# HGRN stage: the projection between the level products in whole chunks at every second place

## What is computed

```
z = RMSNorm_pre(x) @ w_in                      # one projection, 13312 columns
f = lb + (1 - lb) * sigmoid(bf);  k = 1 - f    # per head: bf, bq, bi, bg are 128 columns each of z
S_t = diag(f_t) S_{t-1} + k_t (x) i_t
o_t = S_t^T q_t
y_b = RMSNorm_head(o) * silu(bg)
```

## Time and profile before

| | |
|---|---|
| median of three runs | 1952.8 us |
| profiled execution, whole time | 1953.2 us |
| its span on the core | 1951.4 us |
| TensorE (PE) matmul busy | 1892.8 us, 97% of the span |
| VectorE (DVE) busy | 726.9 us, 37% |
| GpSimd (POOL) busy | 477.7 us, 24% |
| ScalarE (ACT) busy | 354.8 us, 18% |
| TensorE clock granted, mean | 0.989 |

### The profile page before, as it was taken

The page is one execution under the profiler, slowest core; times in us unless marked ns, Lnnn a source line. Parts: engine busy times, 40 slices in busy tenths (PEclk is TensorE's granted clock), DMA queues, the critical chain, the costliest instruction groups (busy, mean ns, idle before and its releaser), DMA issues. The chain is left out here.

```text
span 1951.4 us, 34705 instructions
## 1 busy us (share of the span) xinstructions
PE 1892.8 (97%) x13648; PEld 1827.3 (94%) x13648; DVE 726.9 (37%) x1247; ACT 354.8 (18%) x855; POOL 477.7 (24%) x276
## 2 busy tenths in 40 slices
PE   7999999999999999999999999998999999999796
PEld 6999999999999999999999999998999999999795
DVE  6223123213223325755675665466000412221423
ACT  5121221122022111011011111112111211111221
POOL 2221222221222122222122221232333333332220
PEclk9999999999999999999999999999999999999898
DMA  5424315223333321112122112134322322223512
GB/s 155 118 67 97 100 50 119 84 67 71 104 89 63 92 75 46 54 56 60 39 67 67 34 54 67 35 123 142 99 66 66 104 90 74 75 73 117 181 33 91
DMA packets 245775, 159.18 MB, mean 82 GB/s; under 512 B 35133, under 2 KB 232125, under 8 KB 245692
## 3 DMA queue, kind: packets, MB, share of 16 engines
q1 hardware_dynamic: 207820, 124.16, 22.4%
q10 hardware_dynamic: 37872, 33.79, 5.3%
HBM read 123.48 MB, written 34.44 MB: 81 GB/s over the span
## 5 line engine op out<-in xcount | busy, mean ns | idle before, releaser
L232 PE MATMUL psum<-x_hi,w_hi 128*128 128x384 f32 (+1 forms) x2688 | 886.6, 335 | 20.7 <-DVE x_lo L2126 10.6
L232 PE MATMUL psum<-x_lo,w_hi 128*128 128x384 f32 (+1 forms) x2688 | 868.0, 327 | 0.0
L232 PEld LDWEIGHTS psum<-x_hi,w_hi 128*128 128x128 f32 x2688 | 507.2, 189 | 38.3 <-issue 22.6
L232 PEld LDWEIGHTS psum<-x_lo,w_hi 128*128 128x128 f32 x2688 | 507.9, 189 | 0.0
L232 PE MATMUL psum<-x_hi,w_lo 128*128 128x384 f32 (+1 forms) x2688 | 498.0, 326 | 0.0
L206 POOL CAST w_hi<-w_raw 128x1024 fp32r<-128x1024 f32 (+1 forms) x136 | 145.2, 1068 | 1420.3 <-PE psum L232 1089.2
L232 PEld LDWEIGHTS psum<-x_hi,w_lo 128*128 128x128 f32 x2688 | 451.4, 188 | 0.0
L208 POOL TENSOR_TENSOR w_lo<-w_raw,w_hi 128x1024 fp32r<-128x1024 f32 (+1 forms) x136 | 332.3, 2443 | 10.9
L1569 ACT ACTIVATE a_feature<-psum 128x384 f32<-128x384 f32 (+1 forms) x100 | 45.2, 452 | 355.1 <-PE psum L232 355.1
L1681 DVE TENSOR_TENSOR a_prob<-psum,band 128x128 f32<-128x128 f32 (+1 forms) x64 | 21.5, 378 | 205.2 <-PE psum L1375 203.9
L246 ACT ACTIVATE c_ext<-psum 128x384 f32<-128x384 f32 (+1 forms) x96 | 45.1, 473 | 243.7 <-PE psum L232 234.7
(11 more groups left out here) (226 smaller groups left out, 1792.6 us busy)
## 6 DMA issues: line engine op xcount, KB each, us to landing
w_raw<-in_w_in SPq DMA_DIRECT2D x104, 512.0 KB, 3.9
s_cached<-in_cache_kv_w SPq DMA_DIRECT2D x128, 64.0 KB, 2.6
s_cached<-in_cache_kv_w SPq DMA_DIRECT2D x64, 128.0 KB, 2.4
merged_rows<-c_ext ACTq DMA_DIRECT2D x15, 544.0 KB, 3.0
a_feature<-group_weights SPq DMA_DIRECT2D x12, 512.0 KB, 5.9
spare<-branch_outputs SPq DMA_DIRECT2D x10, 544.0 KB, 6.3
branch_outputs<-b_gate ACTq DMA_DIRECT2D x8, 544.0 KB, 3.1
c_ext<-merged_rows SPq DMA_DIRECT2D x8, 544.0 KB, 3.7
```

Of the source, the lines that this page charges most:

```text
L232: mm = pe.matmul(psum[:, c, 0:n], w[:, s, k, :], x[:, k, t0:t0 + n], start=step is first, stop=step is last)
```

## The change

Only the numbers of halves between the steps of a head change. `counts` is (before, levels, own, out, turn, after).

```diff
                         with pe.Fori(0, BH - 1) as i:
-                            head(i, (1, (1, 1, 1, 1, 2, 1, 1, 1), 2, 4, 5, 3))
-                        head(BH - 1, (1, (1, 1, 1, 1, 2, 1, 1, 1), 3, 5, 6, 0))
+                            head(i, (2, (0, 2, 0, 2, 2, 0, 2, 0), 2, 4, 6, 2))
+                        head(BH - 1, (2, (0, 2, 0, 2, 2, 0, 2, 0), 4, 4, 6, 0))
```

## The result

The changed kernel takes 2019.55 us (median of four runs, 2018.34 to 2024.42), the kernel before 1952.93 us. The forecast was 2006 us with a range of 1996 to 2019. The direction was right. The size was short by 13.5 us of 66.6, and the time lies just above the range. The profiled execution took 2018.34 us, with a span of 2016.5 us.

A forecast was written before the change was run, and what follows sets the result against it. TensorE's in-order list was taken to bound the HGRN stage. Per head 7.17 + 0.35 - 0.70 - 0.19 = 6.63 us, 53 us over eight heads, added to 1953.2 us: forecast 2006 us, range 1996 to 2019.

The forecast's parts named there:

- What bounds the kernel: HGRN stage: TensorE busy 68.91 of 69 us per head, so no slack in which a new stall could vanish.
- Part 1, the four waits: Behind levels 0, 2, 5 and 7 TensorE waits for VectorE's updates: 1.65, 2.06, 1.74, 1.72 us, together 7.17 us per head.
- Part 2, the saved change-overs: Whole-chunk places: four fewer projection visits save 0.70 us per head; the 0.19 us wait ahead of level 6 also disappears.
- Part 3, GpSimd: Levels 4 to 5: GpSimd's subtraction delays update(4), a stall of 0.35 us per head, between 0 and 0.77.
- the first rival, the clock: TensorE's clock falls at the new waits, one fall per head at 1.5 us, 12 us, giving 2018 us; chance 14%.
- The range: Whole time: 1996 us for stalls mis-sized by a fifth, up to 2019 us for one clock fall per head.

The follow-up runs named there:

- levels 0 and 1 alone: Kernel before with nothing behind level 0 and two halves behind level 1, all other places unchanged: 1968.48 us, ratio 1.0084.
- the waits gone: Changed kernel with level products and transposes of k reading constant tiles, so they wait for no update (right data left out): 1944.8 us, ratio 0.9969.
- the kernel with the bare pair 5 and 6: Kernel before with nothing behind level 5 and two halves behind level 6, all other places unchanged: 1984.66 us, ratio 1.0169.
- the kernel with less filler: Changed kernel with three filler matmuls, about 0.6 us, in each of the four bare places: 2009.76 us, ratio 1.0294 to the kernel before.

## Why the prediction was wrong

**What bounds the kernel: right.** TensorE's list had no slack. The length of a head followed the waits and change-overs (levels 0 and 1 alone: 1.38 us more expected, 1.38 found).

**Part 1, the four waits: right.** Timeline of TensorE in the head with full clock, to lay beside the earlier trace rows:

```profile
875.07 1.26 PE L887 MATMUL psum<-b_q_new,b_k_decayed 128*64 128x64 f32 x34
877.88 1.23 PE L887 MATMUL psum<-b_q_decayed,b_k_decayed 128*64 128x32 f32 x34 [1.56 <-DVE b_q_decayed L1040]
883.41 1.24 PE L887 MATMUL psum<-b_q_decayed,b_k_decayed 128*64 128x32 f32 x34
886.62 1.23 PE L887 MATMUL psum<-b_q_decayed,b_k_decayed 128*64 128x32 f32 x34 [1.97 <-DVE b_k_decayed L1053]
891.49 1.12 PE L887 MATMUL psum<-b_q_decayed,b_k_decayed 128*64 128x32 f32 x32
896.93 1.13 PE L887 MATMUL psum<-b_q_decayed,b_k_decayed 128*64 128x32 f32 x32
899.72 1.12 PE L887 MATMUL psum<-b_q_decayed,b_k_decayed 128*64 128x32 f32 x32 [1.66 <-DVE b_k_decayed L1053]
905.16 1.15 PE L882 MATMUL psum<-b_q_decayed,b_k_decayed 128*64 128x64 f32 x16
907.94 1.20 PE L896 MATMUL psum<-ident,b_k_decayed 128*128 128x128 f32 x9 [1.63 <-DVE b_k_decayed L1053]
```

| from start to start | forecast | measured |
|---|---|---|
| level 0 to 1 | 2.84 | 2.81 |
| level 2 to 3 | 3.23 | 3.21 |
| level 5 to 6 | 2.79 | 2.79 |
| level 7 to k | 2.80 | 2.78 |

The idle times in brackets are about 0.08 us shorter than the forecast stalls, since they count from the recorded end of a product and the forecast from 0.07 us before it.

**Part 2, the saved change-overs: right.** In the changed kernel the four distances hold 7.10 us of stall (11.59 less the products' own 4.49), and a head with full clock is 6.19 us longer, so 0.91 us were saved, against 0.70 + 0.19 forecast. With the waits gone the order alone gives 0.55 us per head, or 0.83 without the new wait of `own_states`, against 0.70.

**Part 3, GpSimd: the meeting came, the 0.35 us did not.** Level 4 to 5 took 896.93 - 891.49 = 5.44 us, not 5.8. Timelines of VectorE and of GpSimd, the same head:

```profile
892.66 0.62 DVE L1049 TENSOR_TENSOR b_block_decay<-b_block_decay 128x64 f32<-128x64 f32 x1 [0.36 <-PE psum L887]
893.20 0.68 DVE L1051 TENSOR_TENSOR b_q_decayed<-b_q_decayed,b_block_decay 128x512 f32<-128x512 f32 x1
893.80 2.89 DVE L1053 TENSOR_TENSOR b_k_decayed<-b_k_decayed,b_block_decay 128x512 f32<-128x512 f32 x1
```
```profile
893.28 2.86 POOL L208 TENSOR_TENSOR w_lo<-w_raw,w_hi 128x1024 fp32r<-128x1024 f32 x1
```

The subtraction went in behind L1051 and not ahead of it, so update(4) ended at 896.69, which is just when TensorE came out of the whole chunk. The forecast had the engines' turn wrong by one instruction, and the cover was enough by under 0.1 us (896.69 and 0.15 for the signal make 896.84). Without this term the sum would have been 50 us. It is 49.5.

**The step that failed is the first rival, the clock.** The sum put falls of the clock at nothing; as a rival they had 14% and a price of one fall per head, 12 us. They came, eleven of them, with 16.8 us. The price of one fall was right (1.5 against 1.53 us). The weighing and the number were not. The prediction compared the length of the idle time with the two falls in the trace of before, 2.75 and 2.34 us, and took "shorter than both" and "dense chunks stand around every pair" as reasons against. But two rows with a fall are no lower bound for the idle time that brings one. The second of them had 2.34 us among transposes of 128 columns, and was the nearer one. Around each bare wait stand two products of 32 or 64 columns, and the dense chunks only behind these. The runs show that this neighbourhood counts: 1.33 us idle beside products gave falls in six of eight heads, 1.35 us between dense chunks in none of seven. The Trainium skill, "TensorE: Matmul & The Clock Gate", section "A second HAM failure mode: psum-queue depth-cycling", was quoted for just this case, frequent short idles between groups of matmuls, and the trace here agrees with it: four idle times of 1.56 to 1.97 us in a head, and eleven falls in eight heads.

**The range** ended at 2019 because it took in one fall per head. With four bare places in a head more than one was possible; two in each would be 2006 + 24 = 2030 us. Its ends are also each 1 us beside their own sums (2006 - 11 = 1995, and 2018).

## What to carry to other kernels

Interleaved work between two steps that depend on another engine is cover: before moving it, compare its length with that engine's latency, place by place. A change-over of 0.20 us saved doesn't pay for a bare wait of 1.6 to 2.1 us. When a wait opens on TensorE between light matmuls, price the fall of the clock too, once for each place: here 1.33 us had falls, 0.83 to 0.99 us had none. Look at the work on both sides as well as at the wait. Filler into a bank that is overwritten anyway held the clock here when it left no more than 0.16 us idle, and did not when it left 1.33 us. An earlier start on VectorE can run into a GpSimd instruction, so ask what else runs in the new place.

## What had not been expected of the hardware

A fall of the clock does not come at each equal place. Eight heads with the same 1.56 us of idle time and the same neighbours gave five falls and three without. Falls came in two lengths, about 3.4 us and about twice that. A pair that had none in one kernel (levels 0 and 1 in the changed kernel) had five in another.

Nor does a fall start at a fixed distance from its idle time. By the granted clock, it starts at times before TensorE goes on, by up to 0.7 us (the kernel with the bare pair 5 and 6), and at times up to about 2 us behind (1.8 and 2.0 us in heads 3 and 8 of the kernel with less filler). So the moment at which an idle time comes may decide with its length and its neighbours whether the clock falls. No run here moved an idle time in time and kept all else, so this is not shown. It has a consequence for the counts: the equal places of one kernel aren't eight independent trials, and a number of falls can be read from a trace only roughly, as a share of the places at risk.

GpSimd and VectorE took turns instruction by instruction, but which one of VectorE's three the subtraction came between differed from what the pooling stage had suggested: behind the second here, so that the third took 2.89 us, and behind none before, where the first took 0.94 us.
